# A softmax unit's maximum, exponentials and scaling in two parts, and the scaling ahead of the older unit's norms

## What is computed

```
proj = h @ w_in            # q, k, v of 8 "moba" heads of 64, q, k, v of 4 "diff" heads of 2 x 64, two gates
moba:  p = softmax(q k^T / 8 - slope * distance, causal);            y = p v
diff:  p = softmax(q1 k1^T / 8 + bias) - lam * softmax(q2 k2^T / 8 + bias);   y = rms_norm(p v)
merged = sigmoid(ga) * (ya @ w_branch_a) + sigmoid(gb) * (yb @ w_branch_b)
```

## Time and profile before

| | |
|---|---|
| median of 3 runs | 2052.66 us (2052.63 to 2053.33) |
| the profiled execution | 2050.68 us |
| its span, first to last instruction | 2049.0 us |
| PE busy | 1979.0 us, 97% |
| DVE, ACT, POOL busy | 988.3, 760.0, 281.5 us |
| mean granted PE clock | 0.981 of full speed |
| the stage of the softmax units | about 40 to 290 us of the span |

### The profile page before, as it was taken

One profiled execution on the slowest core, in us unless ns is written; L12 is line 12 of the kernel. 1 busy time (PEld: TensorE's weight loads), 2 busy tenths in 40 slices (PEclk: granted clock), 3 DMA queues, 4 the chain that ended last, 5 costly groups with the idle time before them and its releaser, 6 DMA issues.

```text
span 2049.0 us, 22798 instructions
## 1 busy us (share of the span) xinstructions
PE 1979.0 (97%) x9064; PEld 1602.8 (78%) x9064; DVE 988.3 (48%) x1466; ACT 760.0 (37%) x1148; POOL 281.5 (14%) x273
## 2 busy tenths in 40 slices
PE   8888999989999999899999999999999999999997
PEld 6665788878888887688888878777887788888886
DVE  6655543465333334833333465655754354333334
ACT  5342442343223223432222355556543343223233
POOL 5111000131001011310100130210110011001012
PEclk9998999999999999999999999999999999999998
DMA  5211222423333333233333232111232233333321
GB/s 158 72 52 52 62 67 83 128 73 106 100 93 103 93 91 106 83 100 96 94 102 93 83 93 69 55 52 52 63 100 64 62 103 96 100 92 103 93 88 57
DMA packets 343403, 175.72 MB, mean 86 GB/s; under 512 B 6305, under 2 KB 343298, under 8 KB 343298
## 3 DMA queue, kind: packets, MB, share of 16 engines
q1 hardware_dynamic: 343298, 174.27, 29.2%
HBM read 172.15 MB, written 2.10 MB: 85 GB/s over the span
## 4 chain that ended last, share of the span: by engine, by line
PE 87%; DVE 6%; ACT 3%; issue 2%; POOL 1%; DMA 0%; SPq 0%; DVEq 0%; POOLq 0%; ACTq 0%
PE ps L955 26%; PE ps L959 25%; PE ps L957 25%; PE ps L1005 1%; ACT L L1206 1%; PE ps L1014 1%; PE ps L985 1%; PE ps L1022 1%; PE ps L1038 1%; PE ps L994 1%; POOL TS L1724 1%; PE ps L975 1%; DVE WL L1364 1%; PE ps L1083 1%; POOL X L1750 1%
## 5 line engine op out<-in xcount | busy, mean ns | idle before, releaser
L1364 DVE TENSOR_TENSOR WL<-RAW,WH 128x1024 fp32r<-128x1024 f32 (+2 forms) x336 | 402.4, 1200 | 724.7 <-ACT WH L1140 724.3
L959 PE MATMUL ps<-HL,WH 128*128 128x512 f32 x1728 | 678.9, 393 | 13.2 <-DVE HL L1374 13.0
L955 PE MATMUL ps<-HH,WH 128*128 128x512 f32 x1728 | 687.4, 398 | 0.7 <-ACT HH L1146 0.7
L957 PE MATMUL ps<-HH,WL 128*128 128x512 f32 x1728 | 678.2, 392 | 3.9 <-DVE WL L1364 3.9
L1140 ACT ACTIVATE WH<-RAW 128x1024 fp32r<-128x1024 f32 (+2 forms) x336 | 342.1, 1020 | 542.4 <-PE ps L959 534.4
L959 PEld LDWEIGHTS ps<-HL,WH 128*128 128x128 f32 x1728 | 327.1, 189 | 88.3 <-DVE HL L1374 19.3
L955 PEld LDWEIGHTS ps<-HH,WH 128*128 128x128 f32 x1728 | 327.2, 189 | 76.4 <-issue 6.2
L957 PEld LDWEIGHTS ps<-HH,WL 128*128 128x128 f32 x1728 | 327.5, 190 | 74.1 <-DVE WL L1364 6.5
L955 PE MATMUL ps<-GH,WH 128*128 128x512 f32 x720 | 282.2, 392 | 0.0
L959 PE MATMUL ps<-GL,WH 128*128 128x512 f32 x720 | 280.7, 390 | 0.0
L957 PE MATMUL ps<-GH,WL 128*128 128x512 f32 x720 | 280.3, 389 | 0.0
(11 more groups left out here) (196 smaller groups left out, 1527.8 us busy)
## 6 DMA issues: line engine op xcount, KB each, us to landing
RAW<-in_ffn_w_gu SPq DMA_DIRECT2D x88, 512.0 KB, 3.8
RAW<-in_w_in SPq DMA_DIRECT2D x68, 512.0 KB, 3.8
RAW<-in_ffn_w_down SPq DMA_DIRECT2D x32, 512.0 KB, 4.0
RAW<-in_w_gate SPq DMA_DIRECT2D x22, 512.0 KB, 3.8
RAW<-in_w_up SPq DMA_DIRECT2D x22, 512.0 KB, 3.8
RAW<-in_w_out SPq DMA_DIRECT2D x16, 512.0 KB, 4.1
RAW<-in_mem_w_kv SPq DMA_DIRECT2D x16, 512.0 KB, 3.9
RAW<-in_w_down SPq DMA_DIRECT2D x16, 512.0 KB, 4.1
```

The lines of the kernel that those rows point to most:

```text
L955: e.matmul(bk, wh, xh, start=k == 0, stop=False)
L957: e.matmul(bk, wl, xh, start=False, stop=False)
L959: last = e.matmul(bk, wh, xl, start=False, stop=k == kt - 1)
L1364: e.tensor_tensor(m["WL"][:, s, 0:kt, :], m["RAW"][:, n % NRAW, 0:kt, :], m["WH"][:, s, 0:kt, :].bitcast(F32), ALU.subtract).then_inc(*sg. ...
```

## The change

The maxima, the exponentials and the scaling run in two parts, `PARTS`: blocks 3 and 2, then blocks 1 and 0. The negation of the maxima is a step of its own, `peak`, behind the scores of its part. The exponentials of part 0 are queued at the beginning of stage 2, ahead of the copy of v; those of part 1 at the beginning of stage 3, so behind the `split` of the next weight. The scalings of both parts follow in stage 3. A unit that stands before stage 3 is called ahead of all others (`yield "first"`), so its exponentials of part 1 and its scalings are queued ahead of the older unit's norms. The transposes still wait for part 1 of both halves, as before.

```diff
+PARTS = ((3, 2), (1, 0))
...
         self.scores(u, 3, q, k)
         self.scores(u, 2, q, k)
+        for half in range(2):
+            self.step("peak", (u, half), half, 0)
         yield
+        for half in range(2):
+            self.step("exps", (u, half), half, 0)
         v = self.turn(*vr, ("v", u), 4)
         self.scores(u, 1, q, k)
         self.scores(u, 0, q, k)
...
-        self.step("exps", (u, 0), 0)
-        self.step("exps", (u, 1), 1)
-        yield
-        self.step("scaled", (u, 0), 0)
+        for half in range(2):
+            self.step("peak", (u, half), half, 1)
+        yield "first"
+        for half in range(2):
+            self.step("exps", (u, half), half, 1)
+        for part in range(2):
+            self.step("scaled", (u, 0), 0, part)
+            self.step("combine" if diff else "scaled", (u, 1), 1, part)
+        cb = ("cb", ((u, 1), 1))
         if diff:
-            self.step("combine", u)
-            self.held["L", 0] = (("cb", u),)
-        else:
-            self.step("scaled", (u, 1), 1)
+            self.held["L", 0] = (cb,)
         yield
...
         def step():
-            for g in list(running):
-                if next(g, running) is running:
-                    running.remove(g)
+            for r in sorted(running, key=lambda r: r[1] != "first"):
+                r[1] = next(r[0], running)
+            running[:] = [r for r in running if r[1] is not running]
...
-    def scaled(key, half):
-        st, L = m["ST"][:, half, :], m["L"][half]
-        g.wait_ge(*sg.at("ex", key))
-        e.reciprocal(st[:, 12:16], st[:, 8:12]).then_inc(*sg.inc("rc", key))
-        g.wait_ge(*sg.at("rc", key))
-        for i in range(4):
+    def peak(key, half, part):
+        st, c = m["ST"][:, half, :], PARTS[part][-1]
+        g.wait_ge(*sg.at("lg", (key, c)))
+        e.tensor_scalar(st[:, 4 + c:6 + c], st[:, c:c + 2], -1.0, None, ALU.mult).then_inc(*sg.inc("ng", (key, part)))
+
+    def scaled(key, half, part):
+        st, L, c = m["ST"][:, half, :], m["L"][half], PARTS[part][-1]
+        g.wait_ge(*sg.at("ex", (key, part)))
+        e.reciprocal(st[:, 12 + c:14 + c], st[:, 8 + c:10 + c]).then_inc(*sg.inc("rc", (key, part)))
+        g.wait_ge(*sg.at("rc", (key, part)))
+        for i in PARTS[part]:
             v = L[:, rows_of(i)]
             o = e.tensor_scalar(v, v, st[:, 12 + i:13 + i], None, ALU.mult)
-        o.then_inc(*sg.inc("nw", key))
+        o.then_inc(*sg.inc("nw", (key, part)))
```

More of the change, by code:

```diff
@@ L281, in softmax_unit @@
         if diff:
-            a = self.turn_probs(u, "a", [(1, 0, 0)], ("cb", u))
-            d = self.turn_probs(u, "d", [(1, 1, 0), (1, 3, 0)], ("cb", u))
-            e = self.turn_probs(u, "e", [(1, 2, 0)], ("cb", u))
+            a = self.turn_probs(u, "a", [(1, 0, 0)], cb)
+            d = self.turn_probs(u, "d", [(1, 1, 0), (1, 3, 0)], cb)
+            e = self.turn_probs(u, "e", [(1, 2, 0)], cb)
             self.held["L", 1] = (("tp", (u, "e")),)
@@ L297, in softmax_unit @@
         else:
-            n = [("nw", (u, half)) for half in range(2)]
+            n = [("nw", ((u, half), 1)) for half in range(2)]
             a = self.turn_probs(u, "a", [(0, 0, 0)], n[0])
@@ L333, in pipeline @@
                 done += p() or ()
-            running.append(stages(done))
+            running.append([stages(done), None])
         for p in tail:
@@ L1198, in small_terms, with exps @@
         e.activation(S[:, 26:28], S[:, 24:26], ACT.Exp).then_inc(*sg.inc("st_b", 1))
-    def exps(key, half):
+    def exps(key, half, part):
         st, L = m["ST"][:, half, :], m["L"][half]
         explog()
-        g.wait_ge(*sg.at("ng", key))
-        for i in range(4):
+        g.wait_ge(*sg.at("ng", (key, part)))
+        for i in PARTS[part]:
             v = L[:, rows_of(i)]
             o = e.activation(v, v, ACT.Exp, bias=st[:, 4 + i:5 + i], accum_out=st[:, 8 + i:9 + i])
-        o.then_inc(*sg.inc("ex", key))
+        o.then_inc(*sg.inc("ex", (key, part)))
     def turn_probs(u, name, parts, ev, free):
@@ L1446, in scaled @@
+    def scaled(key, half, part):
[3 more added lines that the diff above has]
+        g.wait_ge(*sg.at("rc", (key, part)))
+        for i in PARTS[part]:
             v = L[:, rows_of(i)]
             o = e.tensor_scalar(v, v, st[:, 12 + i:13 + i], None, ALU.mult)
-        o.then_inc(*sg.inc("nw", key))
-    def combine(u):
-        st, L = m["ST"][:, 1, :], m["L"]
+        o.then_inc(*sg.inc("nw", (key, part)))
@@ L1452, in combine @@
+    def combine(key, half, part):
+        st, L, c = m["ST"][:, half, :], m["L"], PARTS[part][-1]
+        v = st[:, 12 + c:14 + c]
         g.wait_ge(*sg.at("small", 0))
[L1453 to L1458, removed]
@@ L1459, in combine @@
-        for i in range(4):
+        g.wait_ge(*sg.at("ex", (key, part)))
+        e.reciprocal(v, st[:, 8 + c:10 + c]).then_inc(*sg.inc("rc", (key, part)))
+        g.wait_ge(*sg.at("rc", (key, part)))
+        e.tensor_scalar(v, v, S[:, 29:30], None, ALU.mult).then_inc(*sg.inc("cs", (key, part)))
+        g.wait_ge(*sg.at("cs", (key, part)))
+        g.wait_ge(*sg.at("nw", ((key[0], 0), part)))
+        for i in PARTS[part]:
             a, b = L[0][:, rows_of(i)], L[1][:, rows_of(i)]
             o = e.scalar_tensor_tensor(b, b, st[:, 12 + i:13 + i], a, ALU.mult, ALU.add)
-        o.then_inc(*sg.inc("cb", u))
+        o.then_inc(*sg.inc("cb", (key, part)))
@@ L1650, in vector_program @@
                 square_last=square_last, rstd=rstd, normed=normed, split_tile=split_tile, memory_lo=memory_lo, memory_r=memory_r,
-                memory_pair=memory_pair, scores=scores, exps=exps, scaled=scaled, combine=combine, turn_probs=turn_probs,
+                memory_pair=memory_pair, scores=scores, peak=peak, scaled=scaled, combine=combine, turn_probs=turn_probs,
                 head_norm=head_norm, branch=branch, merge_last=merge_last, gate_up=gate_up, down=down, post=post, add_x=add_x,
```

## The result

| | before | changed kernel |
|---|---|---|
| median | 2052.64 us, 4 runs (2051.96 to 2053.33) | 2028.34 us, 4 runs (2025.85 to 2032.4) |
| the profiled execution | 2050.68 us | 2032.4 us |
| its span | 2049.0 us | 2030.3 us |
| mean granted PE clock | 0.981 | 0.986 |

The ratio is 0.9884, with a 95% interval of 0.9866 to 0.9901: 24.3 us less by the medians, where 21.1 were forecast, and 2028.3 us where 2031.6 were. The profiled execution of the changed kernel is the slowest of its four.

What follows compares the result with a forecast made beforehand. PE is busy 97% of the span, so its idle time and low clock set a ceiling of 36.1 us; gains of 15.7 us idle and 5.4 us clock sum to 21.1, giving 2031.6 us, range 2026 to 2041 us.

Steps and rivals of the forecast that it cites:

- DVE 2.0 us earlier: Unit 7: with ACT rounding ahead of part 1's exponentials, DVE is through with projection k at 179.0 instead of 181.0.
- Scaling and combining 4.4 us: Unit 7, DVE ahead of the norms: 4.4 us where 4.55 before, done 1.3 us before PE arrives at the transposes.
- The new wait, 2.0 us in units 6 and 7: PE waits 2.0 us for the next q projection's bank, freed by DVE's projection vr behind the put-off norms.
- Unit 5, 1.8 + 1.5 us: PE waits 1.8 us at the last score product (memory's second bank) and 1.5 at vr's bank; 6.13 becomes 3.3.
- Units 4, 1 and 0, 0.6, 0.5 and 1.5 us: PE's waits shrink: unit 4 from 2.95 to 0.6, unit 1 from 2.05 to 0.5, unit 0 from 3.12 to 1.5.
- The clock, 5.4 us: PE's low clock: of 10.5 us lost, 1.7 stay in each of units 5, 6 and 7, a gain of 5.4 us.
- Unit 3's table: Unit 3, ACT: three table loads of 1.28 us instead of one before part 1 ends; 1.0 us to spare, cost nothing.
- It doesn't do what it says: Rival, chance 0.06: ACT's rounding stays late, DVE doesn't start earlier; 22 of 25.6 us waits stay, 2049.1 us.
- the slower rival: Rival, chance 0.04: WL stays late, units 5 to 7 each wait twice at low clock; 7.6 us more, 2060 us.
- The put-off norms weigh more: Rival, chance 0.26: 1.0 us more wait in each of units 5 to 7, dips as deep as before; 2036.7 to 2040 us.
- the clock never falls: Rival, chance 0.14: PE's remaining waits are too short to lower its clock; gain 26.2 us, 2026.5 us.

Runs made afterwards that it cites:

- the run again: The unchanged changed kernel measured once more against the kernel before: 2029.21 us, ratio 0.9890.
- the run with priority only: Kernel before, exponentials in one part and ahead of the rounding, with only the unit ahead of stage 3 called first: 2047.34 us, ratio 0.9981.
- the run with parts only: Changed kernel without the call-first priority: exponentials and scalings in two parts, older unit's norms still ahead of the scaling; 2042.99 us, ratio 0.9963 against the kernel before.

## Why the prediction was right, by its steps

**DVE 2.0 us earlier.** Right in kind, 0.2 too much. DVE is through with the projection k at 164.40, 5.5 us before PE's transposes (5.7 forecast, 3.7 before). Of the 5.37 us that it waited for ACT 2.20 are left, and it now waits 1.09 for PE, which isn't through with k: 2.1 us less in all. The exponentials start at 157.31, directly behind the square, as the step said.

**Scaling and combining 4.4 us.** Measured 4.36; done 1.2 us before PE arrives, 1.3 forecast. POOL's bias is the reason for the shorter scaling, as the step said: it runs at 173.15, beside the weight tile.

```profile
173.15 1.49 POOL L1740 TENSOR_SCALAR TS<-Dm 128x512 f32<-128x512 f32 x1 [14.80 <-DVE GL L1410]
```

**The new wait, 2.0 us in units 6 and 7.** The mechanism and its place are right, the size is 0.6 too small: 2.60 and 2.59. From the combining's end to PE's start it takes 175.49 - 168.76 = 6.7 us in place of 6.4. The product and the remainder came as forecast (2.9 and 4.3); the tile took 1.52 us in place of 1.2, because the bias that left the scaling alone now stands beside it, which the step had taken as a saving only. The other 0.3 is the scaling's end 0.1 nearer to PE and PE's slot of 2.96 in place of 3.1.

**Unit 5, 1.8 + 1.5 us.** Measured 2.27 + 0.82, 3.1 in place of 3.3: the sum is right by two errors that cancel. DVE of the changed kernel in this slot, beside the earlier trace rows:

```profile
116.77 0.87 DVE L1388 TENSOR_TENSOR TS<-TS 128x256 f32<-128x256 f32 x1 [0.82 <-POOL TS L1732]
117.56 0.86 DVE L1418 SCALAR_TENSOR_TENSOR ML<-ps,G,MH 128x256 fp32r<-128x256 f32 x2
```

The chain over POOL and the memory's second bank is the one of the step; its operation on DVE at L1388, beside POOL's bias from 116.75 on, takes 0.8 us in place of 0.4, and the combining ends 0.2 later. So the first wait is 0.5 longer and the second shorter by what PE has already lost.

**Units 4, 1 and 0, 0.6, 0.5 and 1.5 us.** Measured 0.79, 1.36 and 1.49; units 4 and 0 came as forecast. Unit 1 is the term that was mis-sized: the step gave its scaling 3.2 us, the trace shows 3.9, from 192.58 to 196.44. The step had the two reciprocals more (2.8 + 0.4), but overlooked that POOL's bias, which didn't stand beside this scaling before, now does, and makes each of the two first pairs 0.35 us longer than unit 7's 0.82:

```profile
192.77 1.17 DVE L1454 TENSOR_SCALAR L<-L,ST 128x512 f32<-128x512 f32 x2
192.88 1.73 POOL L1740 TENSOR_SCALAR TS<-Dm 128x512 f32<-128x512 f32 x1 [4.05 <-PE ps L975]
```

The idle time left is 12.0 us, not 9.9, and the gain 13.6 in place of 15.7.

**The clock, 5.4 us.** It gave more. Idle and clock together make the stage shorter by 20.8 us: unit 3's transposes come 20.3 earlier though the stage began 0.5 later (unit 0's transposes at 60.45, before at 60.00). Less the 13.6 that is about 7 us. The step had put a dip of 1.7 us in each of units 5, 6 and 7; there are two, behind unit 5's and unit 7's wait (0.59 from 120.2 to 123.6), and none behind unit 6's. Windows of the q projections behind the transposes of units 6 and 7 in the changed kernel (stretch, us, busy of the engines, granted clock, DMA, GB/s):

```profile
148.80:152.20 3.40, 3.32 (x15) 2.75 (x16) 3.40 (x14) 0.00 (x0) 0.00 (x0) 1.00 0.53 154
175.50:178.90 3.40, 3.40 (x8) 2.72 (x9) 3.40 (x13) 0.00 (x0) 0.00 (x0) 0.51 0.55 154
```

At 0.51, so at 1.2 GHz, eight products are made where fifteen are made at 2.4: 7 x 0.23 = 1.6 us, the size of the 1.7 that the step took for one. So two errors of about 2 us cancel: idle time 2.1 less gained, clock 1.8 more. The sum of the stage is 20.8 where 21.1 was forecast, and that it comes so near is luck. In the profile of the run again the same stretch is 19.6 us shorter, 13.7 of it idle time and 5.9 clock.

**Unit 3's table.** Cost nothing, as forecast. ACT and DVE of the changed kernel in its vr slot:

```profile
242.34 1.28 ACT L1175 ACT_TABLE_LOAD   x1
...
244.87 1.28 ACT L114 ACT_TABLE_LOAD   x1
246.16 0.51 ACT L1213 ACTIVATE L<-L,ST 128x256 f32<-128x256 f32 x1
```
```profile
247.38 0.55 DVE L1454 TENSOR_SCALAR L<-L,ST 128x256 f32<-128x256 f32 x2
```

The first half is scaled at 247.9 and its transposes start at 248.58: 0.65 us to spare, 1.0 forecast. The exponential at 246.16 starts with the end of the load. The Trainium skill (ScalarE: Activation LUTs, What ACT_TABLE_LOAD costs) puts a switch with its drain at about 2.66 us; by this row it is 1.28, and no drain is seen: the sigmoid ahead of the load ends at 244.86, the load starts at 244.87. Nor did PE wait the 3.2 us that the prediction worked out from that figure.

**The median.** The sum fits the stage, while the medians differ by 24.3. The rest, some 3 us, isn't shown to be of the change: in the second comparison the medians differ by 21.8 (2051.05 against 2029.21). The medians of before were 2052.64, 2050.48 and 2051.05 in three groups of runs, and within a group the runs of one kernel lie up to 7.2 us apart. Where behind the stage this spread arises stays open.

**The rivals.** "It doesn't do what it says", no time gained since the rounding stays late, and the slower rival built on the same condition, are excluded by 2.20 in place of 5.37 us. But their arithmetic is that of the run with priority only, in which the rounding does stay late: 22 us of waits and 3.6 us less were forecast by it, 20.3 us of waits and 3.1 us less (2050.48 - 2047.34) came. "The put-off norms weigh more" had part of the truth (0.6 more in units 6 and 7) without the deeper dips; "the clock never falls" was right at one of the three places.

**What the prediction didn't see** is the latency of the norms' own first step, 1.55 us in the run with parts only. It changed nothing in its sum, since the scaling covers it, but the expectation of that run failed by it: 21 us of waits against 14.

## What to carry to other kernels

When one engine works in order through a list that serves two purposes, moving the urgent work ahead moves the wait to whatever stands behind the work put off; ask at once what bank or tile comes free behind it, and when that is wanted. Here putting the older work off by a whole slot, to where its engine is idle, brought the gain from 1.1% to 1.8%; by itself, without the earlier rounding, it gave 1.2%. A step can be placed late if nobody wants its result yet. An operation that waits for another engine's answer is best put behind independent work as long as that answer takes, and cutting a step in parts should be tried against simply queueing the whole step behind the one that others wait for: here the uncut version was as fast.

## What was not expected of the hardware

The same wait doesn't always cost the clock. In the profile above PE's 2.60 us before the q projection in unit 6's slot left the clock full, and the 2.59 us before the one in unit 7's dropped it. In the run of the same kernel again it was the other way round, in the timeline of PE:

```profile
149.97 0.80 PE L962 MATMUL ps<-HH,WH 128*128 128x512 f32 x1 [2.60 <-DVE TS L1404]
150.56 0.63 PE L964 MATMUL ps<-HH,WL 128*128 128x512 f32 x1
...
178.15 0.50 PE L962 MATMUL ps<-HH,WH 128*128 128x512 f32 x1 [2.59 <-DVE TS L1404]
```

So by these two profiles what a wait of this length costs can be given only as a chance of about 1.7 us each; what decides it isn't shown.

DVE's operations between tiles in SBUF were slower beside POOL's bias in most places: by 0.3 us for a weight tile of 128x1024 (1.52 against 1.22), by 0.8 for the scaling of four blocks (2.05 against 1.28) and by 0.35 for that of the two larger ones (1.17 against 0.82). But it isn't always DVE that pays. In two places where they start within 0.1 us of each other the tile took its 1.2 us, and POOL's bias 2.5 to 2.6 us in place of 1.49. One is the second bias in unit 5's slot of the changed kernel (tile at 118.34, 1.21 us), the other stands in unit 1's slot of the kernel before, where the tile starts at 210.78:

```profile
210.84 2.52 POOL L1732 TENSOR_SCALAR TS<-Dm 128x512 f32<-128x512 f32 x1 [4.05 <-PE ps L968]
```

In a third such place, at 28.9 in the kernel before, the tile took 1.67 us and the bias its 1.49. So the cost moves with POOL's bias, wherever its own wait puts it, but which of the two pays isn't settled by these runs.
